# A macaron decoder block in fp32: the first loads on two queues, a sum by halves, and a last piece scaled out of PSUM

## What is computed

```python
def block(x, meta_tokens, ...):
    hs = concatenate([meta, x], axis=1)                       # 16 + 256 tokens
    hs = hs + 0.5 * swiglu(rmsnorm(hs, ffn1_norm), gate1, up1, down1)
    hs = hs + token_mixing(rmsnorm(hs, mix_norm), ...)
    hs = hs + 0.5 * swiglu(rmsnorm(hs, ffn2_norm), gate2, up2, down2)
    return rmsnorm(hs, final_norm)[:, 16:]

def token_mixing(h, ...):                                     # 2 x 1024 channels
    u = h @ w_in + b_in
    y_sc = b_sc * causal_dwconv(c_sc * v_sc, conv_sc_w)       # width 3
    z = a_cf * sigmoid(g_cf)
    z = causal_dwconv(z, conv_cf_w) + conv_cf_b               # width 31
    y_cf = silu(layernorm(z, ln_cf_g, ln_cf_b))               # over 1024 channels
    return concatenate([y_sc, y_cf]) @ w_out
```

## Time and profile before

| | us |
|---|---|
| median of 3 runs | 1853.21 |
| lowest and highest run | 1853.02, 1853.21 |
| profiled execution, device time | 1853.16 |
| its span in the profile | 1851.4 |
| TensorE busy in the span | 1839.4 |
| VectorE busy | 1087.8 |
| ScalarE busy | 902.4 |

### The profile page before, as it was taken

How to read it: one execution, slowest core, us unless ns; L and a number is a source line. 1 busy time by engine, 2 the same in 40 slices (tenths; PEclk the granted TensorE clock), 3 DMA queues, 4 the chain that set the end, 5 groups by cost and what they waited for, 6 DMA issues and landing times.

```text
span 1851.4 us, 34886 instructions
## 1 busy us (share of the span) xinstructions
PE 1839.4 (99%) x14425; PEld 1794.5 (97%) x14425; DVE 1087.8 (59%) x1218; ACT 902.4 (49%) x1151; POOL 5.7 (0%) x16
## 2 busy tenths in 40 slices
PE   9999999999999999999999999999999999999998
PEld 9999999999999999999999999999999999988886
DVE  7555555555554555469899887555555555544454
ACT  6444343343443444359888665444444444444443
POOL 1000000000000000000000000000000000000000
PEclk9999999999999999999999999999999999999999
DMA  6655555555567777755556566666666666665664
GB/s 223 194 180 173 179 177 174 181 175 176 181 173 179 176 178 178 181 173 176 184 184 178 174 206 193 194 192 193 193 193 193 192 194 192 215 192 191 193 188 133
DMA packets 283359, 342.29 MB, mean 185 GB/s; under 512 B 10639, under 2 KB 223985, under 8 KB 283152
## 3 DMA queue, kind: packets, MB, share of 16 engines
q1 hardware_dynamic: 282672, 340.44, 61.7%
q10 hardware_dynamic: 320, 0.53, 0.1%
q0 software_dynamic: 288, 0.19, 0.0%
HBM read 339.02 MB, written 2.10 MB: 184 GB/s over the span
## 4 chain that ended last, share of the span: by engine, by line
PE 98%; DVE 1%; DMA 0%; ACT 0%; SPq 0%; issue 0%; DVEq 0%
PE ps L509 28%; PE ps L511 28%; PE ps L510 28%; PE ps L620 4%; PE ps L622 4%; PE ps L621 4%; DMA x_tok<-in_x 0%; DVE w_same__lo L933 0%; PE ps L471 0%; PE ps L638 0%; DVE zc L1134 0%; PE ps L645 0%; DVE ln_mu L959 0%; SPq L357 0%; PE ps L525 0%; ACT o_tok L918 0%
## 5 line engine op out<-in xcount | busy, mean ns | idle before, releaser
L511 PE MATMUL ps<-x_hi,w_class__lo 128*128 128x272 f32 (+2 forms) x3200 | 901.6, 282 | 0.0
L509 PE MATMUL ps<-x_hi,w_class__hi 128*128 128x272 f32 (+2 forms) x3200 | 900.8, 281 | 0.1
L510 PE MATMUL ps<-x_lo,w_class__hi 128*128 128x272 f32 (+2 forms) x3200 | 900.3, 281 | 0.0
L933 DVE TENSOR_TENSOR w_class__lo<-raw,w_class__hi 128x1024 fp32r<-128x1024 f32 x400 | 489.3, 1224 | 422.3 <-ACT w_class__hi L705 420.9
L705 ACT ACTIVATE w_class__hi<-raw 128x1024 fp32r<-128x1024 f32 x400 | 424.3, 1061 | 564.7 <-PE ps L511 562.5
L510 PEld LDWEIGHTS ps<-x_lo,w_class__hi 128*128 128x128 f32 x3200 | 602.3, 188 | 0.0
L509 PEld LDWEIGHTS ps<-x_hi,w_class__hi 128*128 128x128 f32 x3200 | 601.5, 188 | 0.5 <-PE ps L525 0.5
L511 PEld LDWEIGHTS ps<-x_hi,w_class__lo 128*128 128x128 f32 x3200 | 601.6, 188 | 0.0
L933 DVE TENSOR_TENSOR w_same__lo<-raw,w_same__hi 128x1024 fp32r<-128x1024 f32 x216 | 263.9, 1224 | 261.7 <-ACT w_same__hi L705 261.5
L705 ACT ACTIVATE w_same__hi<-raw 128x1024 fp32r<-128x1024 f32 x216 | 228.4, 1060 | 317.9 <-PE ps L511 169.9
L511 PE MATMUL ps<-a_hi,w_same__lo 128*128 128x272 f32 x640 | 183.4, 287 | 0.0
(11 more groups left out here) (162 smaller groups left out, 1473.8 us busy)
## 6 DMA issues: line engine op xcount, KB each, us to landing
raw<-in_ffn_w_up SPq DMA_DIRECT2D x176, 512.0 KB, 3.6
raw<-in_ffn_w_down SPq DMA_DIRECT2D x176, 512.0 KB, 4.8
raw<-in_ffn_w_gate SPq DMA_DIRECT2D x175, 512.0 KB, 3.5
raw<-in_w_in SPq DMA_DIRECT2D x80, 512.0 KB, 3.5
raw<-in_w_out SPq DMA_DIRECT2D x32, 512.0 KB, 4.9
x_tok<-in_x SPq DMA_DIRECT2D x4, 512.0 KB, 7.9
gain_tok<-in_final_norm SPq DMA_DIRECT2D x1, 1024.0 KB, 5.3
out_y<-o_tok SPq DMA_DIRECT2D x2, 512.0 KB, 2.9
```

Of the source, the lines that this page charges most:

```text
L509: pe.matmul(dst, w_high, act_high, start=first, stop=False)
L510: pe.matmul(dst, w_high, act_low, start=False, stop=False)
L511: return pe.matmul(dst, w_low, act_high, start=False, stop=last)
L933: dve.tensor_tensor(w_lo, raw_rows(phase, s), w_hi.bitcast(F32), ALU.subtract).then_inc(lo_ready, 1)
```

## The change

It has three parts.

1. **First loads.** The two loads of the meta tokens go from the head of SP's queue to ACT's queue, behind the load of `gain_rows`. SP's queue then begins with x. TensorE's 5 idle matmuls between the turns of the meta tokens and of x become 2.
2. **Layer norm.** The sum over 8 tiles of squares, one TENSOR_REDUCE with a strided view, becomes three TENSOR_TENSOR additions: 4 tiles to 4, 2 to 2, and 1 to 1, each waiting for the one before.
3. **Last piece.** DVE no longer multiplies the last piece by 0.5 and the gain while ACT takes the root. The last quarter of the gain is halved once, earlier in the last stage (`gain_halved`); once the inverse root is there, one SCALAR_TENSOR_TENSOR reads the last piece out of PSUM and multiplies it by the inverse root and the halved gain. DVE does this for both halves. In half 1 DVE now has pieces 0 and 3 and ACT pieces 1 and 2; the stores go with them.

```diff
@@ sync @@
-            for h in range(HALVES):
-                meta_half = meta_tokens[:, h * (D // 2):(h + 1) * (D // 2)]
-                sp.dma_start(m_rows[:, h, :],
-                             meta_half.rearrange("t (c p) -> c t p", p=P)).then_inc(meta_loaded, 16)
...
-            for i in range(2):
+            for i, cols in enumerate((out_pieces[0], out_pieces[-1])):
                 sp.wait_ge(o_scaled, SET + i + 1)
-                sp.dma_start(out[0, P:2 * P, out_pieces[i]], o_tok[:, 1, out_pieces[i]]).then_inc(stored, 16)
+                sp.dma_start(out[0, P:2 * P, cols], o_tok[:, 1, cols]).then_inc(stored, 16)
@@ tensor @@
             m.then_inc(meta_turned, 1)
-            keep_warm(5)
+            keep_warm(2)
             for q in (0, 1):
                 turn_pair(q)
@@ scalar @@
             act.dma_start(gain_rows[0:KD, :], ffn1_norm[0].rearrange("(r p) -> r p", p=P)).then_inc(gain_loaded, 16)
+            for h in range(HALVES):
+                meta_half = meta_tokens[:, h * (D // 2):(h + 1) * (D // 2)]
+                act.dma_start(m_rows[:, h, :],
+                              meta_half.rearrange("t (c p) -> c t p", p=P)).then_inc(meta_loaded, 16)
...
             act.wait_ge(last_newton[1], 4)
-            act.wait_ge(tok_read, HALVES * G_D)
-            for cols in out_pieces[2:]:
+            act.wait_ge(tok_read, HALVES * (G_D - 1))
+            for cols in out_pieces[1:3]:
                 act.activation(o_tok[:, 1, cols], o_tok[:, 1, cols], ACT.Copy,
                                scale=tok[:, 3, 1:2]).then_inc(o_scaled_s, 1)
@@ vector @@
                 if g == 0 and h == 0:
                     dve.wait_ge(gain_spread, 16)
+                    dve.tensor_scalar(gain_tok[:, out_pieces[-1]], gain_tok[:, out_pieces[-1]], 0.5, None,
+                                      ALU.mult).then_inc(gain_halved, 1)
...
                 if b == 10:
                     dve.wait_ge(ln_sq, 1)
-                    dve.tensor_reduce(ln_sum[:, :], y_f[:, :, :].rearrange("p c t -> p t c"),
-                                      mybir.AxisListType.X, ALU.add).then_inc(ln_var_sum, 1)
+                    dve.tensor_tensor(y_f[:, 0:4, :], y_f[:, 0:4, :], y_f[:, 4:8, :], ALU.add).then_inc(ln_folded, 1)
+                    dve.wait_ge(ln_folded, 1)
+                    dve.tensor_tensor(y_f[:, 0:2, :], y_f[:, 0:2, :], y_f[:, 2:4, :], ALU.add).then_inc(ln_folded, 1)
+                    dve.wait_ge(ln_folded, 2)
+                    dve.tensor_tensor(ln_sum[:, :], y_f[:, 0, :], y_f[:, 1, :], ALU.add).then_inc(ln_var_sum, 1)
...
-                token_gain(G_D - 1, h)
                 dve.wait_ge(last_sd, h + 1)
                 dve.reciprocal(y, sd).then_inc(steps, 1)
...
-                dve.wait_ge(tok_read, HALVES * (G_D - 1) + h + 1)
-                for cols in out_pieces if h == 0 else out_pieces[:2]:
+                last = out_pieces[-1]
+                dve.wait_ge(tok_read, HALVES * (G_D - 1))
+                dve.wait_ge(gain_halved, 1)
+                for cols in out_pieces[:-1] if h == 0 else out_pieces[:1]:
                     dve.tensor_scalar(o_tok[:, h, cols], o_tok[:, h, cols], scale, None,
                                       ALU.mult).then_inc(o_scaled, 1)
+                dve.scalar_tensor_tensor(o_tok[:, h, last], ps[:, HALVES * (G_D - 1) + h, :], scale, gain_tok[:, last],
+                                         ALU.mult, ALU.mult).then_inc(o_scaled, 1)
```

More of the change, by code:

```diff
@@ L254, in build @@
         ln_sq, ln_var_sum, ln_var_done = sem("ln_sq"), sem("ln_var_sum"), sem("ln_var_done")
+        ln_folded, gain_halved = sem("ln_folded"), sem("gain_halved")
         ln_var, ln_sd, ln_newton, normed = sem("ln_var"), sem("ln_sd"), sem("ln_newton"), sem("normed")
@@ L915, in _ @@
             act.wait_ge(last_newton[1], 4)
-            act.wait_ge(tok_read, HALVES * G_D)
-            for cols in out_pieces[2:]:
+            act.wait_ge(tok_read, HALVES * (G_D - 1))
+            for cols in out_pieces[1:3]:
                 act.activation(o_tok[:, 1, cols], o_tok[:, 1, cols], ACT.Copy,
                                scale=tok[:, 3, 1:2]).then_inc(o_scaled_s, 1)
-            for i, cols in enumerate(out_pieces[2:]):
+            for i, cols in enumerate(out_pieces[1:3]):
                 act.wait_ge(o_scaled_s, i + 1)
@@ L1073, in token_gain @@
                     dve.wait_ge(gain_spread, 16)
+                    dve.tensor_scalar(gain_tok[:, out_pieces[-1]], gain_tok[:, out_pieces[-1]], 0.5, None,
+                                      ALU.mult).then_inc(gain_halved, 1)
                 dve.wait_ge(sums_set, HALVES * g + h + 1)
                 cols = slice(BANK * g, BANK * (g + 1))
[L1076 to L1081, removed]
+                dve.tensor_tensor(o_tok[:, h, cols], o_tok[:, h, cols], gain_tok[:, cols],
+                                  ALU.mult).then_inc(tok_read, 1)
             def conv_adds(phase, b):
```

## The result

| | before | after |
|---|---|---|
| median, us | 1853.19 | 1857.58 |
| lowest and highest | 1852.94, 1855.32 | 1854.87, 1858.64 |
| runs | 16 | 16 |
| profiled execution: span, device time | 1851.4, 1853.16 | 1856.8, 1858.55 |

The ratio is 1.0023, 95% interval 1.0016 to 1.0030: the change makes the kernel 4.4 us slower. The profiled execution of after lies 1.0 us above its median, so the steps read from it are a little larger than the typical ones. In some executions of the experiments, of the kernel before too, 20 us more were taken; in the two profiles of such executions (`e5_sp_holds_rest`, `e7_meta_first_on_act`) they lie between about 1050 and 1620 us, where TensorE has 172 matmuls in 20 us in place of 179, so that the start can be read in them too; why the pace drops, no run shows.

The account below looks back on a forecast made before the run. TensorE was taken as the bound, busy 1839.4 of 1851.4 us. Terms -0.9 (start), 0.0 (layer norm) and -0.25 (end) gave -1.15 on 1853.16, so 1852.01, with 0.05 for the median 1852.05; range 1851.2 to 1853.4.

Parts of the forecast that it names:

- The step that failed: Start: meta tokens on ACT's queue, second issued at 1.93, land at most 3.04 us later, by 4.97.
- part 1: First loads: x issued 1.50 us earlier, less what the meta bytes take from it; -0.9 us.
- Rival (a): Start: meta tokens wait out x's first quarter and land at 6.80; +0.9 there, time 1853.85; 9%.
- the point of decision: Start: late meta tokens delay TensorE's first products once they land after 5.92 us.
- Rival (c): Start: removing three idle matmuls leaves TensorE at slower spacing for another stretch; costs 1.4 us, time 1853.45; 4%.
- Part 2: Layer norm: DVE free some 1.5 us earlier but then idle for TensorE, whose 0.6 us wait stays; 0.0.
- Part 3: End, half 1: reciprocal starts right behind ACT's root, so scalings and last store issue come 0.25 us earlier; -0.25.
- The largest case: Whole kernel: no case reaches 3.7 us; best -2.35, worst +0.9, or +1.4 from the clock.

Follow-up runs that it names:

- e5_sp_holds_rest: The change, but SyncE waits for the meta tokens after issuing the first quarter of x and first weight block; 1854.41 against 1853.44 before.
- e7_meta_first_on_act: The change with gain_rows behind the meta tokens on ScalarE's queue; 1856.65, 0.9 below the change.
- the bridge: The change with 22 more idle matmuls between the turn of gain_rows and the wait for the meta tokens; 1856.88 against the change's 1857.58.

## Why the prediction was wrong

**The step that failed** is in part 1: the meta tokens "on SP ... had landed by 4.57, so at most 3.04 us later. The same from 1.93 is 4.97." That carried a landing time from a queue that had little beside it over to a queue beside a full one. In after the second load was issued at 2.46 and landed 8.40 us later. That it was issued at 2.46 and not at 1.93, since the first took 1.19 to issue on ACT, is a second and smaller miss: with the 3.04 it makes 5.50, still ahead of 5.92. I had weighed the meta rows by the engines' work they need (0.40 to 0.8 us) and asked what they take from x. They took little: x landed 1.76 us earlier, where I had 0.9. The question that mattered was the reverse, what the backlog takes from them. The runs give it in four points, for loads whose last was issued between 2.4 and 2.7: landed by 4.7 with nothing beside, at 7.0 with x and a block, at 8.3 (8 KB) and 10.9 with the full list. The rule that I quoted from the Trainium skill, "DMA: Bandwidth & Descriptors", section "Issuing engines are not separate DMA queues", that DMAs of different issuers interleave on the same engines, agrees with this trace, where both queues move packets in the microseconds shown. It says nothing of equal delay: q10 has 11 packets to 121 in one of them.

**Rival (a)** had the late meta tokens and the point of decision right (a landing after 5.92), but its size wrong: 6.80 by letting the meta rows wait for x alone. SP had x, the first blocks and more of x queued, and the meta rows waited beside all of them. Its price of +0.9 at the start was +5.7 in the profile. It had 9%.

**Rival (c)**, the clock, came true too, not by the three idle matmuls but as a consequence of the wait: 0.7 us of the loss in the medians, 1.3 in the profiles (the bridge). The removed idle matmuls themselves may cost 0.3; that they cost nothing was not shown. The wait and the clock add up, and no case of mine had them in one; the range ended 4 us too low, by the wait above all.

**Part 2** held: 2.33 us in place of 3.90, all of it turned into idle time of VectorE (0.36 became 1.85), the 0.6 us wait still there. **Part 3** held: 0.24 in the chain as predicted (0.25), with 0.2 more behind the last issue, which I had not counted; I had expected the stores to take from it. The profile of the third part alone has the same 0.5 us behind the root, so the gain is the third part's in the profiles, though the medians do not show it apart. The kernel with these two alone is at 1852.65 where I had 1852.95.

**The largest case.** I had written that no case reaches 3.7 us; the change lost 4.4. The start can lose more than it can win: TensorE's order puts the meta tokens ahead of all, so any delay of theirs beyond 5.92 passes on in full, while the gain ended at 1.5.

Not settled: by what rule the turns are divided between the queues, and whether the rows wait at the engines or on the way to them; and why the landing varies (10.86 in the profile of the change, 10.12 in that of its first part alone). The times of the change lie between 1854.87 and 1858.64, and no trace was kept of the short ones.

## What to carry to other kernels

A small load that something early waits for should not go to a second queue beside a deep backlog: at or near the head of the full queue it was there in time, in a queue of its own it waited with most of the other's backlog. Price a moved load by what will be queued beside it until it lands, not by the engines' work in its bytes, and look for the first consumer in program order on the engine that bounds. To win at the start here, cut the issues ahead of x (one DMA for two: first product 0.72 us earlier than in the profile of before, 0.47 earlier than in that of parts 2 and 3 alone) or put x first and the small loads behind it in the same queue (1.35 and 1.10 us earlier). With parts 2 and 3 these versions have medians of 1852.31 and 1852.37 against 1853.14, the lowest of all that were run, though their intervals do not exclude no change, and parts 2 and 3 alone are at 1852.65.

## What the runs showed of the hardware

- 8 KB by ACT's queue landed 1.6 us after issue with little else running, 3.0 when issued together with the first load of x, and 5.6 beside SP's full queue.
- Two loads of 64 KB, their second issued at about 2.4 us: landed by 4.7, at 7.0 or at 10.9, with nothing, 1 MB or the whole list on SP's queue. With the whole list a second profile has 10.1.
- Eight turns took 1.10 us in before, 1.97 with three idle matmuls fewer ahead of them, both at a granted clock of 1.00, and 1.91 in after at 0.50. So the spacing of the matmuls says more than the granted clock.
- In after TensorE had run no matmul since 4.6 us; its granted clock was 0.76 in the stretch from 8.0 and 0.50 from 8.5 to 15 us, through the turns, and 1.00 again at 15.5.
- One DMA with both halves of the meta tokens took 0.80 us to issue, the same as one with a single half. The same single half took 1.19 to 1.27 us to issue on ACT.
